# Spreading a per-token column as rows over all partitions: TensorE transposition of the broadcast column in place of a product with the identity

## What is computed

```python
def rms_norm(x, g):
    xf = x.astype(jnp.float32)
    y = xf * lax.rsqrt(jnp.mean(xf * xf, axis=-1, keepdims=True) + EPS)
    return (y * g.astype(jnp.float32)).astype(x.dtype)
```

## Time and profile before

| | |
|---|---|
| time, median of 3 runs | 1423.56 us (1421.67 to 1424.01) |
| time of the profiled execution | 1422.82 us |
| its span | 1420.8 us |
| TensorE (PE) busy | 1397.1 us, 98% |
| VectorE (DVE) busy | 838.2 us, 59% |
| ScalarE (ACT) busy | 602.9 us, 42% |
| GpSimd (POOL) busy | 165.5 us, 12% |

### The profile page before, as it was taken

How to read it: one execution, slowest core, us unless ns; L and a number is a source line. 1 busy time by engine, 2 the same in 40 slices (tenths; PEclk the granted TensorE clock), 3 DMA queues, 4 the chain that set the end, 5 groups by cost and what they waited for, 6 DMA issues and landing times.

```text
span 1420.8 us, 17484 instructions
## 1 busy us (share of the span) xinstructions
PE 1397.1 (98%) x6892; PEld 1138.4 (80%) x6892; DVE 838.2 (59%) x1245; ACT 602.9 (42%) x921; POOL 165.5 (12%) x124
## 2 busy tenths in 40 slices
PE   7999999999999999999999999999999999999898
PEld 5777777878888888888888888787778888888686
DVE  5556565745343797624776365645464657687774
ACT  5254433433235554423444255434353544344461
POOL 3300010212212300000000221000002111211030
PEclk9999999999999999999999999999999999999999
DMA  6221322222352333332333324421134333221141
GB/s 231 80 83 52 98 63 75 71 64 91 103 164 88 133 105 104 106 102 83 95 101 119 95 71 137 132 60 60 60 104 149 89 104 107 75 60 46 45 140 68
DMA packets 37265, 135.39 MB, mean 95 GB/s; under 512 B 4400, under 2 KB 5056, under 8 KB 36672
## 3 DMA queue, kind: packets, MB, share of 16 engines
q1 hardware_dynamic: 37184, 134.28, 29.8%
HBM read 127.97 MB, written 6.29 MB: 94 GB/s over the span
## 4 chain that ended last, share of the span: by engine, by line
PE 94%; DVE 2%; ACT 1%; DMA 1%; issue 0%; SPq 0%; POOL 0%; DVEq 0%; ACTq 0%; POOLq 0%
PE ps L203 93%; PE ps L207 1%; DMA cv<-in_cvec 1%; ACT WH L187 1%; DMA raw<-in_wall 1%; SPq L210 0%; DVE TT L162 0%; DVE WL L150 0%; ACT SS L200 0%; DVE SS L174 0%; POOL SQS L150 0%; DVE HL L162 0%; DVE PB L174 0%; DVE TH L150 0%; DVE PB L162 0%
## 5 line engine op out<-in xcount | busy, mean ns | idle before, releaser
L203 PE MATMUL ps<-HH,WH 128*128 128x512 f32 x1088 | 439.6, 404 | 9.3 <-DVE WL L150 8.9
L203 PE MATMUL ps<-HH,WL 128*128 128x512 f32 x1088 | 425.2, 391 | 0.0
L203 PE MATMUL ps<-HL,WH 128*128 128x512 f32 x1088 | 424.5, 390 | 0.0
L150 DVE TENSOR_TENSOR WL<-raw,WH 128x1024 fp32r<-128x1024 f32 x222 | 283.2, 1280 | 78.5 <-ACT WH L187 77.3
L187 ACT CAST WH<-raw 128x1024 fp32r<-128x1024 f32 x222 | 231.5, 1044 | 147.9 <-PE ps L203 130.0
L203 PEld LDWEIGHTS ps<-HH,WH 128*128 128x128 f32 x1088 | 204.9, 188 | 59.2 <-DVE WL L150 8.9
L203 PEld LDWEIGHTS ps<-HH,WL 128*128 128x128 f32 x1088 | 204.6, 188 | 44.3
L203 PEld LDWEIGHTS ps<-HL,WH 128*128 128x128 f32 x1088 | 205.0, 188 | 41.6 <-issue 1.7
L150 POOL TENSOR_TENSOR SQS<-SQS,SQ 128x512 f32<-128x512 f32 x54 | 83.3, 1543 | 743.0 <-ACT SQ L200 727.8
L203 PE MATMUL ps<-PH,WH 128*128 128x512 f32 x424 | 168.7, 398 | 1.1 <-DVE TT L150 1.1
L203 PE MATMUL ps<-PH,WL 128*128 128x512 f32 x424 | 165.7, 391 | 0.0
(11 more groups left out here) (216 smaller groups left out, 1456.8 us busy)
## 6 DMA issues: line engine op xcount, KB each, us to landing
raw<-in_wall SPq DMA_DIRECT2D x222, 512.0 KB, 3.6
kept<-PW SPq DMA_DIRECT2D x2, 2048.0 KB, 9.2
PWR<-kept SPq DMA_DIRECT2D x2, 2048.0 KB, 7.7
X<-in_xT SPq DMA_DIRECT2D x8, 256.0 KB, 5.9
X<-in_xT SPq DMA_DIRECT2D x4, 512.0 KB, 5.5
out_T<-X SPq DMA_DIRECT2D x8, 256.0 KB, 2.0
pe<-in_pT SPq DMA_DIRECT2D x2, 512.0 KB, 4.4
DM<-in_dm SPq DMA_DIRECT2D x1, 640.0 KB, 4.2
```

What stands on the lines that cost most here:

```text
L150: return self.put(None if self.e is None else self.e.tensor_tensor(out, x, y, op))
L203: return self.put(None if self.e is None else self.e.matmul(out, l, r, start=start, stop=stop, skip_group_check=True))
```

## The change

`pe_row` calls the helper for transpositions in place of the helper for products. The stationary operand (the column, broadcast with step 0 to 128x128), the moving operand (`ident`), the output and the semaphores stay as they are.

```diff
@@ pe_row
             p.wait_ge(S.ident, "ident")
             p.wait_ge(S.dve, *key)
             for t in range(4):
-                p.matmul(s[:, t * P:(t + 1) * P], col[:, t:t + 1].to_broadcast([P, P]), ident, True, True)
+                p.transpose(s[:, t * P:(t + 1) * P], col[:, t:t + 1].to_broadcast([P, P]), ident)
             p.then_inc(name, *consumed)
```

## The result

| | before | after |
|---|---|---|
| time, median | 1422.62 us (4 runs, 1421.39 to 1424.01) | 1415.07 us (4 runs, 1414.51 to 1415.32) |
| profiled execution: time, span | 1422.82, 1420.8 us | 1414.51, 1412.5 us |

The ratio is 0.9946, 95% interval 0.9929 to 0.9963: the change makes the kernel 7.5 us faster by these runs. Forecast were 7.4 us, and 1416.2 us as the time. The tenths of the 7.5 therefore mean little.

A forecast was written before the change was run, and what follows sets the result against it. TensorE's instruction list was taken to bound the kernel. 14 rows x 0.46 plus 2 x 0.50 gave 7.4 us, taken from the three-run median 1423.56 to forecast 1416.2 us, range 1413.5 to 1419.7.

The forecast's parts named there:

- What bounds the kernel: Whole program: the kernel ends when TensorE, busy 98%, has gone through its list, on which the changed instructions stand.
- Start to start in place of duration: At the 16 rows: time TensorE is held, 0.81 to 0.35 us between blocks, saves 0.46; behind a wait, 0.50.
- Step 0: In the rows' transpositions: a stationary column broadcast with step 0 costs nothing measurable, so 0.109 us a step holds.
- Rival 1: At the rows: transposing a broadcast takes two passes, no gain, 1423.6 us; with loads as limit, 1419.6; chance 0.05.
- Waits: TensorE's total of waits stays as it is, and those at the last attention, 3.3 us in four, don't grow.
- Rival 2: At the last attention: longer waits for transposed weights take up 6.9 us, time 1423.1; partial loss about 1420; chance 0.04.
- What lies beside other work: nothing of it: At all 16 rows: none of the saving is hidden beside other engines' work, so the full 7.4 us counts.
- The clock: Half-clock stretch at 1350.70 to 1354.10 us costs 1.7 us; whether it comes again could not be told.
- Rival 3: Around the rows: TensorE's clock falls, 1.7 us each, slower from five falls, 1443 us with 16; chance 0.04.
- without it the gain is 9.1: If the half-clock stretch near 1350 us does not return, the gain is 9.1 us; with a second one, 5.7.
- TensorE's busy time: Whole program: the changed profile would show TensorE's busy time down by about 7.4 us to 1390.
- the loads hide behind the passes: In the rows: weight loads of 140 or 190 ns leave the 0.109 us step unchanged; uncovered, the gain is 4.0 us.

## Why the prediction was right

- *What bounds the kernel.* TensorE's list, nearly without cover. Time taken from the rows came through (7.0 to 7.5 us of 7.4 forecast, 0.3 being lost in one wait), time put into them came through (15.0 of 14.2), and so did time put behind them. This was the step on which all else rested, and it was read from the chain and the few waits, not from the 98% alone.
- *Start to start in place of duration.* 0.46 and 0.50 us a row were forecast from neighbours in the trace of before; 0.455 and 0.50 are what the changed rows show. Read as durations, 4 x 0.272 us, the same operation would have been forecast as a loss. The Trainium skill, "TensorE: Matmul & The Clock Gate", Part 4: PE-mode transpose, gives some 275 ns in a kernel's context. As a duration this agrees with the trace's 272 ns for float32; as time that the engine is held it does not, since four hold it for 0.354 us in all.
- *Step 0.* That the broadcast costs a transposition nothing was taken from the loads of the product. The run with an ordinary operand shows it (1414.90 against 1415.07 us). The loads themselves are 136 ns, and 140 with the ordinary operand. Rival 1 is out.
- *Waits.* Rival 2, the gain taken up by waits, came about only in a small part with 7.4 us in 16 pieces: not at the last attention, where it was looked for, but at `gqks`, 0.3 us. "What lies beside other work: nothing of it" was too strong by that much. With a further 13.4 us taken from TensorE in 30 pieces, nearly 4 were lost in waits that grew. The gain per microsecond becomes smaller as VectorE's chains come close.
- *The clock.* Rival 3 is out for groups of 4 and 8 transpositions (64 more of them, granted clock 1.00 through all the changed kernel's work up to its last microseconds, in which TensorE is done). Here one size was off: "without it the gain is 9.1" counted the half-clock stretch at 1.7 us, a little more than the 1.6 of its passes, and at its full cost, where only some 0.6 came back, since a wait of 0.7 us appears in its place. The stretch occurred in the one profiled execution of the kernel before and in none of the other eight profiles, so that it says nothing on the change.
- *TensorE's busy time* fell by 9.0 us, not 7.4; the difference is the passes of that same stretch, which counted double in the trace of before.
- *The time.* 1416.2 us were forecast and 1415.07 measured. The gain was right; the base was 1.5 us too high, as the median of three runs (1423.56) against 1422.10 in 24. 7.4 less the 0.3 lost at `gqks` is 7.1, which fits the 7.0 against the 24 runs; that the result's own difference, 7.5, comes as close to 7.4 is partly luck, for its median of before, 1422.62, is 0.5 above theirs.

## What to carry to other kernels

When the chain ends on TensorE and its waits are few, count its passes, not its instructions or their durations: at 128 columns a plain float32 product is two of 0.11 us, a float32 transposition one, and what a group holds the engine for is read from its first start to the start of what follows it. A product with the identity that only moves or spreads data can be a transposition, broadcast operand and all. Before taking more from the same engine, look for its waits, the small ones and those that nearly occur, and for where the chain that ends each of them begins: a saving that lies between that beginning and the wait is lost in part or whole, while one ahead of the beginning, or in it, moves the chain too and comes through.

## What the runs showed that had not been expected

- With 128x128 weights, a pass of one or two columns holds TensorE as long as a pass of 128: 0.112 us (sums, eight in 0.81 us from their start to the next block, the first pair nearer together) against 0.111 (rows). So rounding the operands of products that are one column wide saved 0.112 us for each pass that it removed. What holds a pass so narrow is not shown: the number of columns does not, and each pass has a load of 128 columns of weights, which these runs never took away alone. The prediction's "the loads hide behind the passes" is shown only in so far as the loads' duration, 136 or 190 ns, makes no more than 0.02 us in a row between blocks.
- A stretch of half clock, 3.4 us long, cost about 0.6 us at the end and not the 1.6 that its passes took longer, because VectorE used it to catch up.
- The start of the first row differed by 0.7 us between two executions of the same instructions, from the landing of one weight unit; of the 8.3 us by which the two profiled spans differ, that much is no effect of the change. In the nine profiles this row starts between 34.1 and 35.4 us, so a few tenths between the spans of two single executions need no edit to explain them.
